# Two copies of a decay row, a diagonal masked in place by GpSimd, and halves added one unit later

## The reference

```python
def fox_attend(q, qc, qpos, k, v, kc, kpos):
    scale = q.shape[-1] ** -0.5
    s = jnp.einsum('bqhd,bkhd->bhqk', q, k) * scale
    s = s + jnp.transpose(qc, (0, 2, 1))[..., None] - jnp.transpose(kc, (0, 2, 1))[:, :, None, :]
    s = jnp.where((kpos[None, :] <= qpos[:, None])[None, None], s, -jnp.inf)
    p = jax.nn.softmax(s, axis=-1)
    return jnp.einsum('bhqk,bkhd->bqhd', p.astype(v.dtype), v)

def fox_prompt(q, k, v, logf):
    c = jnp.cumsum(logf.astype(F32), axis=1)     # the decay row: one value a key, for each head
    # 8 blocks of 128 queries, each against all keys up to its own diagonal block
```

## Time and profile before

| | us |
|---|---|
| median of 3 runs | 1266.69 (1266.52 to 1270.23) |
| the profiled execution | 1267.65 |
| its span | 1265.5 |
| PE busy over the span | 1151.2 (91%) |
| DVE busy | 735.0 (58%) |
| ACT busy | 415.3 (33%) |
| GpSimd busy | 171.7 (14%) |
| first score of the attention on DVE | starts at 539.70 |
| first work of the output projection on PE | starts at 755.11 |

### The profile page before, as it was taken

The page is one execution under the profiler, slowest core; times in us unless marked ns, Lnnn a source line. Parts: engine busy times, 40 slices in busy tenths (PEclk is TensorE's granted clock), DMA queues, the critical chain, the costliest instruction groups (busy, mean ns, idle before and its releaser), DMA issues.

```text
span 1265.5 us, 21223 instructions
## 1 busy us (share of the span) xinstructions
PE 1151.2 (91%) x7607; PEld 683.3 (54%) x7607; DVE 735.0 (58%) x1732; ACT 415.3 (33%) x905; POOL 171.7 (14%) x189
## 2 busy tenths in 40 slices
PE   6999999999999999879899999999639999999970
PEld 4686776867866455656566665445333333333320
DVE  6935665855745012568888764346764444334876
ACT  4322524424323010347777762213200110111431
POOL 0122031210311000310000000000010111112233
PEclk8999999999999999979999999999758999999995
DMA  9751030130201303311620015400476968586984
GB/s 292 263 139 27 27 77 3 45 57 20 84 1 52 121 17 51 115 38 32 168 62 4 15 51 182 140 34 17 171 257 209 345 252 299 200 266 250 349 320 156
DMA packets 127315, 164.77 MB, mean 130 GB/s; under 512 B 32257, under 2 KB 101201, under 8 KB 127222
## 3 DMA queue, kind: packets, MB, share of 16 engines
q1 hardware_dynamic: 112070, 109.91, 28.8%
q0 software_dynamic: 15152, 53.60, 11.6%
HBM read 226.35 MB, written 36.47 MB: 208 GB/s over the span
## 4 chain that ended last, share of the span: by engine, by line
PE 78%; DVE 12%; DMA 4%; issue 3%; ACT 1%; POOL 1%; SPq 1%; DVEq 0%; POOLq 0%; ACTq 0%
PE act L729 18%; PE vec L1350 11%; PE vec L764 8%; PE vec L1076 8%; PE vec L739 5%; PE act L999 4%; PE vec L985 4%; PE vec L780 2%; PE act L1363 2%; PE vec L1363 2%; DMA arena<-x_rows,arena 2%; PE act L1011 2%; DVE arena L2091 2%; DVE arena L2107 2%; PE act L1024 1%
## 5 line engine op out<-in xcount | busy, mean ns | idle before, releaser
L729 PE MATMUL act<-arena 128*128 128x352 f32 x768 | 237.2, 464 | 0.3 <-issue 0.3
L729 PEld LDWEIGHTS act<-arena 128*128 128x128 f32 x768 | 143.3, 190 | 76.8 <-issue 1.8
L1350 PE MATMUL vec<-arena 128*64 128x512 f32 x768 | 174.5, 606 | 2.3 <-DMA arena<-in_exp_w 2.3
L1076 PE MATMUL vec<-arena 128*128 128x512 f32 x256 | 112.9, 594 | 0.8 <-DVE arena L2116 0.8
L1350 PEld LDWEIGHTS vec<-arena 128*64 128x64 f32 x768 | 53.8, 139 | 103.5 <-issue 101.8
L764 PE MATMUL vec<-arena 128*128 128x512 f32 (+1 forms) x256 | 100.3, 546 | 0.0
L1598 ACT ACTIVATE arena<-arena 128x640 f32<-128x640 f32 (+15 forms) x128 | 81.4, 642 | 11.4 <-DVE arena L2091 10.7
L2441 DVE TENSOR_SCALAR arena<-arena 128x256 f32<-128x256 f32 x24 | 7.3, 302 | 133.6 <-ACT arena L1695 133.6
L999 PE MATMUL act<-arena 128*128 128x128 f32 x440 | 65.3, 285 | 17.8 <-DVE arena L2107 16.9
L2091 DVE CUSTOM_DVE_ANT_0 arena<-vec,arena 128x128 f32<-128x128 f32 (+6 forms) x168 | 69.1, 431 | 18.9 <-PE vec L985 8.1
L1589 ACT COPY arena<-act 128x128 f32<-128x128 f32 (+3 forms) x176 | 63.9, 434 | 47.7 <-PE act L999 47.5
(11 more groups left out here) (461 smaller groups left out, 1858.4 us busy)
## 6 DMA issues: line engine op xcount, KB each, us to landing
arena<-in_exp_w SPq DMA_DIRECT2D x192, 512.0 KB
arena<-in_exp_w SPq DMA_DIRECT2D x48, 1024.0 KB
y_rows<-arena POOLq DMA_DIRECT2D x24, 512.0 KB, 6.3
arena<-in_w_in SPq DMA_DIRECT2D x16, 512.0 KB, 6.7
arena<-in_x_prompt SPq DMA_DIRECT2D x8, 512.0 KB, 6.2
x_spill<-arena POOLq DMA_DIRECT2D x8, 512.0 KB, 2.9
arena<-x_spill SPq DMA_DIRECT2D x8, 512.0 KB, 4.8
arena<-in_cache_fox_kv SPq DMA_DIRECT2D x16, 256.0 KB, 3.4
```

The lines of the kernel that those rows point to most:

```text
L729: last = mm(bk[:, 0:n], W[k % 2][:, c, m * P:(m + 1) * P], xT[:, c, a:a + n], start=c == 0, stop=c == NC - 1)
L1076: last = mm(bk[:r], src, Wo[half][:, c, :], start=c == 0, stop=c == NC - 1)
L1350: last = mm(gu_bank[p][o], xgT[p][:, c, o], Wgu[:, slot, c, :], start=c == 0, stop=c == NC - 1)
```

## The change

It does three things. The decay row of a head is kept in two copies, `fox_rows[h % 2][0]` and `[1]`, in the place of `cumf` and `foxdiag`; query block i reads copy i % 2, whose diagonal block has the mask added in place. So the bias of a fox chunk is one piece. Second, GpSimd keeps the copies right: `mask_diagonal(h, i)` adds the mask to block i of copy i % 2 ahead of its use, and once DVE has added the scores of fox i, block i is restored from the other copy, since later query blocks need it unmasked. SP loads each row twice; for head 0 GpSimd makes the second copy. Third, `add_halves` moves from the end of an even step to the middle of the next odd step, behind `scores(it)` and ahead of `normalise(it-1)`.

```diff
-    cumf, foxdiag = [z.take(1024) for _ in range(2)], [z.take(SEQ, 8) for _ in range(2)]
+    fox_rows = [[z.take(SEQ) for _ in range(2)] for _ in range(2)]
...
         if kind == "fox":
-            off = min(n, i * P - a)
-            whole = [(0, off, cumf[h % 2][:, a:a + off])] if off > 0 else []
-            return whole + ([(n - P, P, foxdiag[h % 2][:, i, :])] if a + n == L else [])
+            return [(0, n, fox_rows[h % 2][i % 2][:, a:a + n])]
...
-            e.dma_start(cumf[h % 2], bcast(decay_rows[8 * h:8 * h + 8], SEQ)).then_inc(...)
+            for copy in fox_rows[h % 2]:
+                e.dma_start(copy, bcast(decay_rows[8 * h:8 * h + 8], SEQ)).then_inc(...)
...
             if d % 2 == 0:
-                e.wait_ge(*E.at(("foxdiag", h)))
+                e.wait_ge(*E.at(("diagonal masked", h, i)))
+                if i >= 2:
+                    e.wait_ge(*E.at(("row restored", h, i - 2)))
...
+            if it >= 5 and it % 2:
+                add_halves(it - 4)
             if 2 <= it <= n:
                 normalise(it - 1)
-            if it >= 4 and it % 2 == 0:
-                add_halves(it - 3)
+        add_halves(n - 1)
...
+        def mask_diagonal(h, i):
+            row = fox_rows[h % 2][i % 2][:, i * P:(i + 1) * P]
+            tt(row, row, C["diagmask"], ALU.add).then_inc(*E.done(("diagonal masked", h, i)))
...
-                    tt(foxdiag[h % 2], cumf[h % 2].rearrange("p (t k) -> p t k", t=8), C["diagmask"]..., ALU.add)
+            if d == 0:
+                e.wait_ge(*E.at(("cumf", 0)))
+                e.tensor_copy(fox_rows[0][1], fox_rows[0][0]).then_inc(*E.done())
+                e.wait_ge(*E.own())
+                mask_diagonal(0, 0)
+                mask_diagonal(0, 1)
+            if kinds[0] == "fox" and i + 2 < 8:
+                mask_diagonal(h, i + 2)
+                e.wait_ge(*E.at(("scores", d, 0)))
+                used, plain = (fox_rows[h % 2][x][:, i * P:(i + 1) * P] for x in (i % 2, 1 - i % 2))
+                e.tensor_copy(used, plain).then_inc(*E.done(("row restored", h, i)))
             if d % 16 == 9 and h + 1 < H:
                 e.wait_ge(*E.at(("cumf", h + 1)))
-                tt(foxdiag[(h + 1) % 2], cumf[(h + 1) % 2]..., C["diagmask"]..., ALU.add)
+                mask_diagonal(h + 1, 0)
+                mask_diagonal(h + 1, 1)
```

More of the change, by code:

```diff
@@ L584, in load_decay @@
         def load_decay(h):
-            e.dma_start(cumf[h % 2], bcast(decay_rows[8 * h:8 * h + 8], SEQ)).then_inc(*E.moved(f"cumf{h % 2}_in", ("cumf", h)))
+            for copy in fox_rows[h % 2]:
+                e.dma_start(copy, bcast(decay_rows[8 * h:8 * h + 8], SEQ)).then_inc(*E.moved(f"cumf{h % 2}_in", ("cumf", h)))
         load_decay(1)
@@ L2053, in first_decay_rows @@
             e.wait_ge(*E.own())
-            c_ = cumf[h % 2]
+            c_ = fox_rows[h % 2][0]
             for g in range(2):
@@ L2597, in _ @@
                 e.memset(Sw[i % 2][1][:, 8 * (i % 2) + 7:], 0.0).then_inc(*E.done(("tail cleared", h + 1, i % 2)))
[L2598 to L2601, removed]
+            if d == 0:
[9 more added lines that the diff above has]
+                e.tensor_copy(used, plain).then_inc(*E.done(("row restored", h, i)))
             if d % 16 == 9 and h + 1 < H:
                 e.wait_ge(*E.at(("cumf", h + 1)))
-                tt(foxdiag[(h + 1) % 2], cumf[(h + 1) % 2].rearrange("p (t k) -> p t k", t=8), C["diagmask"].unsqueeze(1).to_broadcast([P, 8, P]), ALU.add).then_inc(*E.done(("foxdiag", h + 1)))
+                mask_diagonal(h + 1, 0)
+                mask_diagonal(h + 1, 1)
         E.stage("p5")
```

## The result

The changed kernel took 1292.3 us (median; 1288.1 to 1298.8), the kernel before beside it 1268.5: 1.019 times as long, 95% interval 1.014 to 1.0239. In a second comparison it was 1.0204 (1.0173 to 1.0235). So it is 24 to 26 us slower. The forecast was slower by 13, with a range up to 1288.

What follows compares the result with a forecast made beforehand. It took a cycle between PE and DVE, without slack for PE's delays, as the bound. 12.8 - 3.4 + 4.0 - 0.35 = +13.05 us on the profiled 1267.65 gave 1280.7, so 1279.7 for the runs; range 1268 to 1288.

Steps and rivals of the forecast that it cites:

- Part 2: Fox values on PE: the halves' bank comes free later, 0.78 us a cycle, 5.5 a head; with part 1, +12.8.
- the 0.6 of slack: Taken off part 2 per head: 0.5 in the last cycle, where PE idles before fox 7's transposes, and 0.1 small slack.
- The signs named for it: PE held at fox values by the halves' addition 0.5 to 0.8 us; a head lasts 53 to 54 instead of 50.
- Part 1: Fox scores on DVE: one piece of 384 takes 0.48 us instead of 0.73 for two; gains 1.6 a head, 6.4 in all.
- Faster: Rival at the halves' bank: it is free in time in spite of the order; -6.15 us, 1260.5; chance 0.12.
- Part 3: GpSimd's three wide mask additions leave the loop, and with them stalls of DVE: -3.4 us.
- Part 4: GpSimd's short masks and copies stall DVE around L2101 and L2107: +4.0 us, ends 0 and 11.
- port rival: Short GpSimd instructions meet DVE at nearly every unit: part 4 is 11 us instead of 4, 1286.7; chance 0.12.
- Part 5: Start: first score waits for a GpSimd copy and one short mask, 2.0 us against 2.35: -0.35 (-0.8 to +0.5).
- swap of idle time: Rival: PE alone bounds the cycle, new stalls replace its present idle time; +8.5 in place of 12.8, 1275.4; chance 0.16.

Runs made afterwards that it cites:

- Late: The changed kernel's order, halves added behind the next odd unit's scores; the changed kernel itself took 1292.3 us, again 1293.8.
- early: The changed kernel with the addition of halves back at its old place, the end of the even step: 1261.1 us, ratio 0.995.
- filled kernel: The changed kernel with three extra 128x128 matmuls on PE ahead of its wait for the halves' bank: 1281.0 us, ratio 1.0108 (with six: 1295.3).
- smaller ring: The changed kernel with two banks instead of three for the transposes; with the addition early and one bank for the halves: 1287.7 us, ratio 1.0149.

## Why the prediction was right and wrong

The direction and the mechanism were right. The size wasn't: 13 us forecast, 24 to 26 measured, and the time lay above the range. Two steps failed: the delay of the bank, 4 us too small, and the clock of PE, which the sum had at nothing.

**Part 2, the bank: right mechanism, 4 us too small.** Late and early differ by 6.3 us a head at full clock (55.34 and 49.07), by 5.9 without short masks (54.25 and 48.37), by 5.8 on the kernel before; I had 4.9. The rows of i = 1 and 7 say why. I put 0.04 us, which no row gave, between the end of the addition and PE's start; it was 0.15. DVE's scores stood 0.93 instead of 0.82 at i = 1. So the values are 0.95 and 0.93 later than before, not 0.71 and 0.80. Seven cycles by 0.94, less the 0.6 of slack, are 6.0 a head; over four heads, less the first cycle, 23.6 in place of 19.2. The signs named for it came: PE is held before the values for 0.8 to 1.1 us (0.5 to 0.8 forecast), and a head at full clock lasts 55.3 (53 to 54 forecast).

**What was missing: the clock, 5 to 12 us.** No step of mine asked what PE's new idle time does to PE's own speed. A head before has PE busy 46.1 of 50.0 at clock 1.00; late it has 46.4 of 55.3, and there the clock fell in five of the six inner heads of the two profiles. A head at 0.94 takes 57.1 to 58.2 against 55.3, so 2 to 3 each. The filled kernel shows that it hangs on the idling: with the wait filled the clock is up and the ratio 1.0108 against 1.019 and 1.0204, so 10 to 12 us by the medians, 5 and 11 in the attention of the profiled executions. With the larger delay the sum is 13.05 + 4.4 = 17.5; the measured 24 to 26 leave 7 to 9 for the clock, the larger part of the error.

**Part 1, one piece: right.** 0.48 as forecast. Part 1 alone wasn't run, but the early kernel without short masks comes near to it: its inner head takes 48.37 against 50.00 before, 1.6 less as forecast. Together with parts 3 to 5 I had -6.15 with the addition early, the rival "Faster" at 1260.5; measured 1261.1. That rival failed for the reason given against it, not by its sizes.

**Part 3, the wide masks: 3.4 of PE's wait gone as forecast**, in time 2 us with an interval from 4.4 to nothing.

**Part 4, the short masks: right early, not late.** Their stall is 4.0 us of DVE's time in both orders; of the kernel's time it is 2.8 by the heads and 5.2 by the medians early (forecast 4.0). Late it was 11 to 13: 1.1 a head at full clock, and the rest goes with the clock, which was down in the inner heads with the masks and up without them. How a microsecond more of idle time a head does that isn't shown. My port rival (11 us) had the size, but from more meetings, which there weren't.

**Part 5: about right.** DVE waited 1.46 for GpSimd at the start instead of 3.65, but its first score came at 540.57 instead of 539.70: GpSimd's copy could begin only at 538.86. From there it took 1.71, against a forecast of 2.0. The start itself varies by more than the part is worth: in the second profile of the same kernel the first score came at 538.12. It decides nothing.

**The swap of idle time** happened in part: the old wait fell by 9.5 us. It didn't cap the loss as that rival had it: DVE now waits too, 43.3 us in place of some 8, so the two engines take turns where they used to overlap.

What stays open: why one late head keeps the clock up and the next, with the same instructions, doesn't. The share of idle time alone doesn't say it: with the smaller ring and the addition early a head was as long as a late one and the clock stayed at 1.00.

```profile
607.87:663.19 55.32, 47.09 (x426) 32.78 (x425) 41.06 (x166) 38.70 (x116) 5.81 (x16) 1.00 0.40 125
```

Nor is a filler needed: without short masks, late, the clock was 1.00 in both inner heads shown with PE busy 46.4 of 54.2. I have no rule for it, only that filling the wait held it up in the inner heads of both kernels where it was tried.

## What to carry to other kernels

An addition that empties the only bank of a ring belongs ahead of everything that the other engine doesn't wait for; here a delay of 0.94 us a cycle cost 6 us a head, and one that left PE a wait of 0.19 cost 1. Where a change adds idle time to the matrix engine in short pieces, price its clock as well: give it a rival of its own, with the length of the same stretch at both levels. And look which vector instruction a small GpSimd one runs beside: the same 0.74 us a unit cost 2.5 to 5 us beside the scaling and nothing that could be measured beside the addition and the scores.

## What was not expected of the hardware

The clock fell although no wait of PE for DVE before the transposes or the values was longer than 1.2 us, and three matmuls of no use in each cycle made the changed kernel 10 to 12 us faster by the medians. A 128x1024 copy on GpSimd takes 1.14 us where the addition of that size takes 2.35; at 128x128 it is 0.29 and 0.45. Taking one of three banks from the transposes' ring cost 25 us, as much as the whole change.
